# A two-layer hybrid decoder trunk on one core: halved squares at the start, shifted attention steps, moved norms, and gathered rows turned on VectorE

## What is computed

```python
for i in range(DEPTH):                                   # DEPTH = 2
    h = rms_norm(x, norm_mix_g[i])
    x = x + token_mixing(h, ...)                         # conv, pooling, windowed attention, gates
    h = rms_norm(x, norm_ffn_g[i])
    if i % 2 == 0: x = x + swiglu(h, w_gu, w_down, D_FF)
    else:          x = x + moe_ffn(h, moe_router, moe_w_gu, moe_w_down)
    h = rms_norm(x, norm_ple_g[i])
    x = x + sigmoid(h @ ple_w_gate[i]) * (p[i] @ ple_w_proj[i])
return rms_norm(x, final_norm_g)
```

## Time and profile before

| | |
|---|---|
| median of 3 runs | 1207.21 us (1206.4 to 1207.79) |
| profiled execution | 1207.06 us |
| its span, first to last instruction | 1205.3 us |
| mean granted TensorE clock | 0.998 of full |
| busy: PE, PEld, DVE, ACT, POOL | 1192.5, 994.3, 898.3, 717.9, 110.4 us |
| busy DVE in 1000 to 1100 us (experts) | 88.6 us |
| moved in 1000 to 1100 us | 387 GB/s |

### The profile page before, as it was taken

The page is one execution under the profiler, slowest core; times in us unless marked ns, Lnnn a source line. Parts: engine busy times, 40 slices in busy tenths (PEclk is TensorE's granted clock), DMA queues, the critical chain, the costliest instruction groups (busy, mean ns, idle before and its releaser), DMA issues.

```text
span 1205.3 us, 15422 instructions
## 1 busy us (share of the span) xinstructions
PE 1192.5 (99%) x5955; PEld 994.3 (82%) x5955; DVE 898.3 (75%) x875; ACT 717.9 (60%) x688; POOL 110.4 (9%) x134
## 2 busy tenths in 40 slices
PE   9999999999999999999999999999999999999997
PEld 7997788888888888998788888888888888888875
DVE  5877755655555558667756788998888888888996
ACT  7437434544443437446544677777777777777765
POOL 3720000200000002420000100000000000000301
PEclk9999999999999999999999999999999999999999
DMA  9965455776667646645455599999999999999970
GB/s 333 327 205 171 156 175 175 236 255 230 210 225 242 231 153 195 202 145 185 164 175 175 163 369 367 390 370 391 380 388 381 389 379 390 378 391 379 393 285 36
DMA packets 160827, 324.91 MB, mean 270 GB/s; under 512 B 6936, under 2 KB 48176, under 8 KB 160768
## 3 DMA queue, kind: packets, MB, share of 16 engines
q1 hardware_dynamic: 156000, 308.57, 73.1%
q0 software_dynamic: 4480, 14.51, 3.3%
q10 hardware_dynamic: 288, 1.05, 0.3%
HBM read 314.14 MB, written 9.96 MB: 269 GB/s over the span
## 4 chain that ended last, share of the span: by engine, by line
PE 92%; DVE 4%; ACT 3%; issue 1%; POOLq 0%; POOL 0%; DVEq 0%; ACTq 0%
PE ps L2027 24%; PE ps L1773 17%; PE ps L1775 17%; PE ps L1774 17%; PE ps L2014 11%; DVE split L1106 2%; ACT split L704 1%; PE ps L1994 1%; PE ps L1789 1%; PE ps L2130 1%; PE ps L1840 1%; PE ps L1971 1%; PE ps L1851 0%; PE ps L1810 0%; ACT split L753 0%
## 5 line engine op out<-in xcount | busy, mean ns | idle before, releaser
L1106 DVE TENSOR_TENSOR split<-raw,split 128x2048 fp32r<-128x2048 f32 x271 | 621.6, 2298 | 196.5 <-ACT split L704 193.9
L704 ACT ACTIVATE split<-raw 128x2048 fp32r<-128x2048 f32 x274 | 524.8, 1916 | 274.3 <-PE ps L1775 203.4
L2027 PE MATMUL ps<-split,br 128*128 128x512 f32 x1344 | 317.5, 392 | 0.5 <-DVE split L1106 0.3
L2027 PEld LDWEIGHTS ps<-split,br 128*128 128x128 f32 x1344 | 249.5, 188 | 55.0 <-DVE split L1106 2.0
L1773 PE MATMUL ps<-split,hT 128*128 128x512 f32 (+1 forms) x600 | 234.2, 390 | 0.9 <-DVE split L1106 0.4
L1774 PE MATMUL ps<-split,hT 128*128 128x512 f32 (+1 forms) x600 | 230.3, 384 | 0.0
L1775 PE MATMUL ps<-split,hT 128*128 128x512 f32 (+1 forms) x600 | 230.3, 384 | 0.0
L2014 PE MATMUL ps<-split,hT 128*128 128x512 f32 x672 | 159.5, 392 | 0.1
L2014 PEld LDWEIGHTS ps<-split,hT 128*128 128x128 f32 x672 | 124.8, 188 | 27.9 <-issue 1.7
L1773 PEld LDWEIGHTS ps<-split,hT 128*128 128x128 f32 x600 | 112.8, 188 | 27.5 <-issue 3.2
L1775 PEld LDWEIGHTS ps<-split,hT 128*128 128x128 f32 x600 | 112.7, 188 | 22.6
(11 more groups left out here) (295 smaller groups left out, 971.5 us busy)
## 6 DMA issues: line engine op xcount, KB each, us to landing
raw<-moe_w_gu_dram SPq DMA_DIRECT2D x96, 1024.0 KB
raw<-moe_w_down_dram SPq DMA_DIRECT2D x56, 1024.0 KB
raw<-w_in_dram SPq DMA_DIRECT2D x45, 1024.0 KB
raw<-ffn_w_gu_dram SPq DMA_DIRECT2D x28, 1024.0 KB
raw<-moe_w_gu_dram SPq DMA_DIRECT2D x32, 512.0 KB
raw<-ffn_w_down_dram SPq DMA_DIRECT2D x14, 1024.0 KB
raw<-w_branch_dram SPq DMA_DIRECT2D x12, 1024.0 KB
raw<-w_out_dram SPq DMA_DIRECT2D x8, 1024.0 KB
```

The lines of the kernel that those rows point to most:

```text
L704: act.activation(buffer(t, 0), raw[:, t % RAW, :], ACT.Copy).then_inc(hi, 1)
L1106: dve.tensor_tensor(buffer(t, 1), raw[:, t % RAW, :], buffer(t, 0).bitcast(F32), ALU.subtract).then_inc(lo, 1)
L2027: ins = pe.matmul(ps[:, 5 if kind == "up" else 4, :], xe[:, sl, 4 * part + k, :], slot(t, sr, 512)[:, k, :], start=part + k + m == 0, stop ...
```

## The change

1. **Start.** Both blocks' squares are taken in two halves; ACT takes half of the first block's, DVE the other half and both halves of the second. PE's idle matmuls are 6 and 2 instead of 11 and 4. ACT splits the third tile before the two evictions, and PE's third tile waits for the first eviction alone.
2. **Attention.** The third unit's scores stand in `upool`, and DVE's mask no longer waits for turned pieces. Turning, copying and the products with the values come one tile later, and so do the splits of the attention's result.
3. **Gate of layer 0.** ACT's four squares come earlier, between the turns, and a Sigmoid of one column stands where they were.
4. **Experts.** POOL copies `Y` in an order of quarters into `spare` and stores it from there; ACT's stores are gone. The lists go through memory, so that each quarter of the partitions has the whole list, and give the rows of a view of `y_rows` in quarters of 1 KB. Each gather is four, one for each quarter of the columns. At tile 15 DVE turns the rows with four block transposes into `rows_turned`, in SBUF, and PE no longer does.

```diff
-ATT, ATT_HALF, ATT_OUT = 1, 8, 12
+ATT, ATT_HALF, ATT_OUT = 1, 9, 13
-AT_ROUTE, AT_TURN, AT_NEXT = 3, (4, 10, 16, 18), 16
+AT_ROUTE, AT_TURN, AT_NEXT = 3, (4, 10, 16, 18), 15
...
         def scores_of(u):
-            return Y[:, u % 2, :]
+            if u == 2:
+                return upool[:, :, 16:]
+            return Y[:, u, :].rearrange("p (h n) -> p h n", n=ATT_UNITS[u][3])
...
+            def store_parts(b):
+                pool.wait_ge(y_ready, 2 * (NB * NTH_Y[4] + b) + 2)
+                for a in range(4):
+                    ins = pool.tensor_copy(y_part[b][:, a].rearrange("p (k j) -> p k j", k=KD),
+                                           Y[:, b, :].rearrange("p (k a j) -> p k a j", k=KD, a=4)[:, :, a])
+                chain(ins)
+                pool.dma_start(y_rows[b * P:(b + 1) * P, :], spare[b]
+                               ).then_inc(y_stored, 16)
...
             def rows_of(s, i):
-                pool.indirect_dma_start(rows_in, None, y_rows[:, :],
-                                        bass.IndirectOffsetOnAxis(slot_tok[:, i:i + 1], 0)
-                                        ).then_inc(rows_landed[s], 16)
+                for part in range(4):
+                    pool.indirect_dma_start(rows_in[:, part * 256:(part + 1) * 256], None, y_parts[:, :],
+                                            bass.IndirectOffsetOnAxis(slot_row4[:, part, i:i + 1], 0)
+                                            ).then_inc(rows_landed[s], 16)
+            def move_lists(s):
+                pool.wait_ge(slots_ready[s], 1)
+                pool.dma_start(list_rows[:, :], slot_first[:, :]).then_inc(lists_moved, 16)
+                pool.wait_ge(lists_moved, 80 * (s - 1) + 16)
+                for a in range(4):
+                    pool.dma_start(slot_part[a * 32:(a + 1) * 32, :, :],
+                                   list_rows.rearrange("(t i) e -> i t e", t=4)).then_inc(lists_moved, 16)
+                pool.wait_ge(lists_moved, 80 * s)
+                chain(pool.tensor_scalar(slot_row4[:, :, :], slot_part[:, :, :], quarter[:, 0:1], None, ALU.add))
...
-            def store_y(b):
-                act.wait_ge(y_ready, 2 * (NB * NTH_Y[4] + b + 1))
-                act.dma_start(y_rows[b * P:(b + 1) * P, :], Y[:, b, :]).then_inc(y_stored, 16)
...
+            split_hi(2)
             for b in range(NB):
                 hold_proj(b)
...
+                if l == 0:
+                    for nh in range(2):
+                        mean_square(0, nh, x_ffn, nh + 1)
                 turn_hi(4 * l + 3, (1,) if l else (0, 1))
                 split_gate_hi(l, 1)
+                if l == 0:
+                    for nh in range(2):
+                        mean_square(1, nh, x_ffn, nh + 3)
...
                 if l == 0:
-                    for b in range(NB):
-                        for nh in range(2):
-                            mean_square(b, nh, x_ffn, 2 * b + nh + 1)
+                    act.activation(nmx[:, 0, 0:1], power[:, :], ACT.Sigmoid)
...
             def mask_scores(l, u):
                 dve.wait_ge(s_done, 3 * l + u + 1)
-                if u == 2:
-                    dve.wait_ge(pr_turned, 6 * l + 2)
...
+            def turn_rows(s, n):
+                dve.wait_ge(rows_landed[s], 64 * n)
+                for part in range(4):
+                    ins = dve.transpose(rows_turned[:, :, part * 32:(part + 1) * 32],
+                                        rows_in[:, part * 256:(part + 1) * 256].rearrange("p (k j) -> p k j", k=KD))
+                ins.then_inc(gathered[s], 2)
...
+                    if j == AT_NEXT and not last:
+                        turn_rows(s, s + i)
                     if j in AT_MUL:
...
-                        if 0 <= at - ATT - 5 < 6:
-                            take_probs(l, at - ATT - 5)
+                        if 0 <= at - ATT - 6 < 6:
+                            take_probs(l, at - ATT - 6)
...
-            def turn_rows(s, n):
-                pe.wait_ge(rows_landed[s], n)
-                for k in range(KD):
-                    ins = pe.transpose(ps[:, 2 + k // 4, k % 4 * P:(k % 4 + 1) * P],
-                                       rows_in[:, k * P:(k + 1) * P], ident[:, :])
-                    if k % 4 == 3:
-                        ins.then_inc(gathered[s], 1)
...
-            idle_work(11, 0, ones, ones)
+            idle_work(6, 0, ones, ones)
...
-                if l == 0:
-                    pe.wait_ge(proj_out, NB)
+                    pe.wait_ge(proj_out, 1)
                 for b in range(l, NB):
                     keys_values(t0 + 2, b)
+                if l == 0:
+                    pe.wait_ge(proj_out, NB)
...
-                        if at - ATT - 6 in (0, 2, 4):
-                            att_values(l, (at - ATT - 6) // 2)
-                        if 0 <= at - ATT - 4 < 6:
-                            att_turn(l, at - ATT - 4)
+                        if at - ATT - 7 in (0, 2, 4):
+                            att_values(l, (at - ATT - 7) // 2)
+                        if 0 <= at - ATT - 5 < 6:
+                            att_turn(l, at - ATT - 5)
```

## The result

The changed kernel takes 1198.25 us (median of five runs, 1198.02 to 1198.76), the kernel before 1207.21 (1206.4 to 1207.79). The ratio is 0.9927, with a 95% interval of 0.9916 to 0.9937: 8.96 us less, where 9.35 were forecast. The profiled execution took 1198.02 us, its span is 1196.3 us.

What follows compares the result with a forecast made beforehand. PE was taken as the bound. Gains of 6.1, 2.5, 0.65 and 0.6 us less losses of 0.3 (routing) and 0.2 (stream) gave -9.35 us, 1197.9 us; range 1195.8 to 1203.0.

Steps and rivals of the forecast that it cites:

- What bounds the kernel: Whole kernel: PE is the bound; a microsecond is won only where PE works less or waits less.
- The transposes' price and cover: Experts, tile 15: four DVE transposes take 1.4 us, leaving 0.4 us before PE wants tile 17's split.
- No loss per expert: Experts: DVE's added transposes cost PE nothing, under thin cover; the next split starts 0.6 us late without harm.
- The experts' period: Experts: DVE's transposes from first to seventh expert 6 x 59.3 us apart, where PE's were 6 x 60.2.
- What speaks against it: Experts: turning rows of 128x1024 costs PE 0.87 us and will cost DVE 1.4 us.
- Attention: Attention, both layers: PE's waits for `sc` and `Y` go, 0.65 + 0.6 us per layer, 2.5 us in all.
- loads from memory set the first product: Start: so halved squares and fewer idle matmuls are set at nothing, 0 to -0.5 us.
- Routing: Routing: POOL's copies take 11.6 us with issue 0.6 more, pushing DVE splits; PE loses 0.3 us (0 to 1.5).
- the largest risk: First expert's gather: lands 732.5, asked for at 733.1, covered by 1 us, set at nothing; coming late has chance 0.26.
- the weight stream: Rival, experts: 382 to 389 GB/s is the limit, the period stays, 6.1 us are lost, 1204.0 us; chance 0.08.
- the quarters: Rival, experts' gathers: each waits until the one before has landed; 25 us lost, 1222 us; chance 0.04.
- equal wait: Rival, attention: the shift does not help, the wait returning at the values' second half; 1200.4 us; chance 0.03.

Runs made afterwards that it cites:

- turned_twice: The kernel after with each of DVE's four transposes per expert made twice, the first into memory nobody reads; 1204.98 us, ratio 0.9981.
- att_only: The kernel before with the attention part of the change alone; 1205.5 us, ratio 0.9983.
- idle_only: The kernel before with 6 and 2 idle matmuls instead of 11 and 4, nothing else; 1208.22 us, ratio 1.0009.
- start_only: The kernel before with the changed start alone (halved squares, 6 and 2 idle matmuls, third tile's split ahead of the evictions); 1207.75 us, ratio 1.0005.
- tokens_spread: copies_later with DVE's work on weights, rows and picks spread over the second, third and fourth experts; 1197.37 us, ratio 0.9914.
- copies_later: The kernel after with POOL's eight copies held back until DVE has built the four lists; 1197.65 us, ratio 0.9922.
- whole_rows: The kernel after with one gather of 4 KB rows per expert instead of four of 1 KB, lists not sent through memory; 1197.78 us, ratio 0.9924.
- start_more_idle: The kernel before with the changed start alone, but still 11 and 4 idle matmuls; 1206.62 us, ratio 0.9996.
- experts_only: The kernel before with the experts' part of the change alone; 1202.88 us, ratio 0.9962.

## Why the prediction was right, point by point

| term | forecast | measured in the trace | |
|---|---|---|---|
| rows not turned on PE | -6.1 | -6.1 | gone from PE |
| transposes on DVE, weight stream | +0.2 | +0.65 | mis-sized: 0.24 us in the second expert, about 0.07 in each other |
| attention | -2.5 | -1.84 | mis-sized |
| layer 0's gate | -0.65 | -0.78 | held |
| start, third tile | -0.6 | -0.63 | held |
| start, first product | 0 to -0.5, set at 0 | -0.73 | mis-sized |
| routing | +0.3 | +0.25 | held |
| end | 0 | +0.17 | drift |
| sum | -9.35 | -9.0 | |

- *What bounds the kernel* held: PE gained what it did less or waited less, and DVE's additional 10 us cost it only 0.65 us.
- *The transposes' price and cover* held best: 1.4 forecast and 1.34 measured, 0.4 us left and 0.38 measured, and turned_twice showed that this cover is real and no larger. "No loss per expert" did not hold in the second expert, where DVE already had 4 us of other work; the earlier trace rows were of the fifth.
- *The experts' period*: the forecast of 59.3 us came out partly by luck. Its starting point, 60.2 us, is the distance from the first of eight transposes in the first expert to the last of eight in the seventh; from first to first it is 60.05 (737.3 and 1097.6 us). Less 0.87 that gives 59.2, and 59.28 was measured, 0.1 more: the loss in the row of the transposes.
- *What speaks against it*, that DVE takes longer than PE to turn the rows, did not decide. DVE needs 1.34 us where PE needed 0.87, and the run is faster since only PE's time was on the path. In turned_twice, where DVE's extra 1.34 us find too little cover, a later expert takes PE 60.0 us, no less than with its own transposes (59.9).
- *Attention* was sized wrongly, by 0.7 us: I took the whole gap above ordinary spacing as lost, and from the wait for `Y` I took off nothing at all, while part of each gap is the change from tiles to short matmuls itself (0.98 us per layer won, not 1.25). A further 0.14 us per layer PE gives back behind attention (att_only).
- *The start*: "loads from memory set the first product" was the step that failed. The earlier trace rows began at 20 us; the chain of the kernel before has the idle matmuls (L1810) at its very start, that of the kernel after (second fence) a load of weights:

```profile
1.06 4.56 PE ps L1810 x22
...
6.95 4.35 PE ps L2130 x10
```

```profile
3.68 7.22 DMA raw<-w_in_dram
```

  Of the other kernels with 6 and 2 idle matmuls, idle_only, start_only and tokens_spread have another load there and copies_later has the idle matmuls again: with so few of them, loads and idle matmuls end close together (the longest wait of PE for a load there is 1.09 us, in idle_only).
- *The total*: the errors of attention and of the first product, 0.7 us each, cancelled in the sum, and the other errors leave 0.35 us. That the sum came so close is luck; the first product alone begins within a band of 1.0 us.
- *Routing*: the loss was right, the account behind it was not. I priced POOL's copies by an addition (0.68 us); four free copies take 1.43, 0.36 each. And I set the blocked ones at three of 2.7 us; it was one, of 2.10 us. So the first gather, which I called the largest risk at 1 us of cover (chance 0.26), had 8 us. What PE lost in the routing, 0.25 us, came from a small DVE operation held up beside the copies (1.43 us instead of 0.28; copies_later), which the prediction did not have, and not from pushed splits.
- *The rivals*: the weight stream is not the limit (the later experts take PE 59.1 us instead of 59.9, at 389 GB/s instead of 387), and gathers in pieces of 1 KB do not slow it (389 GB/s from 1000 to 1100 us in the kernel after and in whole_rows); the quarters do not come in series (1.8 to 3.1 us from one to the next); no equal wait returned in attention.

## What to carry to other kernels

Work may move from the engine that bounds the kernel to one that does it more slowly (here from 0.87 us on PE to 1.34 us on DVE), as long as it is put where that engine's next two deadlines leave room (0.38 us here): measure the cover by doing the moved work twice (PE then waited 0.9 us per expert in turned_twice), and spread other small work away from it (1.0 us in the trace of tokens_spread). Price an operation by a row of the same kind (a free copy took 0.36 us, where the addition had 0.68), and subtract from a wait what the change of work costs without any wait (here 0.32 and 0.20 us). A difference of less than 0.1% between two kernels is best read from paired starts of the bounding engine's instructions, stage by stage, since the starts of the whole program's work spread by a microsecond (first products at 13.56 to 14.59 us with 6 and 2 idle matmuls).

## What was not expected of the hardware

- PE stopped for 1.8 to 2.0 us without a releaser, 1165 us behind an edit that removed 14 of its instructions (idle_only, start_only), with transfers on the instruction queues 1.5 to 2.8 us before it goes on; with the 14 back (start_more_idle) it does not stop, though such transfers are there. In the trace of start_only the granted clock then fell to 0.50 for some 3 us, in that of idle_only it did not; by the mean clocks (0.996 or 0.997 in five of eleven of start_only, 0.997 in three of eleven of idle_only) it fell in some executions of both.
- Beside POOL's copies a DVE operation of 0.28 us took 1.43 us (kernel after) and one of 0.17 us took 1.12 (copies_later), while splits of 2.28 us took 2.28 to 2.42 (both).
- DVE's block transposes of 128x256 follow each other in 0.335 us (kernel after).
- The first product of a split tile begins within a band of 0.5 us (11 and 4 idle matmuls) to 1.0 us (6 and 2). With 11 and 4 this is mostly the time of the 22 idle matmuls, 4.56 to 5.06 us: the spacing of PE's short matmuls goes from 0.21 to 0.11 us at 5.0 us in the kernel before and at 6.1 us in experts_only, while the granted clock reads 1.00.
